# HGRN scores with two levels per product, and the order of the stage around them

## What is computed

```python
def step(S, xs):
    qq, kk, lf, vv = xs
    A = jnp.cumsum(lf, axis=2)
    o_inter = jnp.einsum('bhtd,bhde->bhte', qq * jnp.exp(A), S)
    rel = jnp.where(tri[:, :, None], A[:, :, :, None, :] - A[:, :, None, :, :], -jnp.inf)
    att = jnp.einsum('bhtd,bhsd,bhtsd->bhts', qq, kk, jnp.exp(rel))
    o_intra = jnp.einsum('bhts,bhse->bhte', att, vv)
...
ck = jnp.einsum('bcpgd,pde->bcge', kc[:, cidx] + pe_k[:, None, :], w_ck)
cv = jnp.einsum('bcpgd,pde->bcge', vc[:, cidx] + pe_v[:, None, :], w_cv)
```

## Time and profile before

| | |
|---|---|
| runs, median of 3 | 485.43 us (485.16 to 486.59) |
| the profiled execution | 485.57 us |
| its span, first to last instruction | 483.8 us |
| TensorE busy | 475.2 us, 98% |
| TensorE's weight loads | 463.9 us, 96% |
| VectorE | 343.2 us, 71% |
| ScalarE | 264.6 us, 55% |
| GpSimd | 159.1 us, 33% |
| granted TensorE clock | 0.998 |

### The profile page before, as it was taken

One profiled execution on the slowest core, in us unless ns is written; L12 is line 12 of the kernel. 1 busy time (PEld: TensorE's weight loads), 2 busy tenths in 40 slices (PEclk: granted clock), 3 DMA queues, 4 the chain that ended last, 5 costly groups with the idle time before them and its releaser, 6 DMA issues.

```text
span 483.8 us, 9621 instructions
## 1 busy us (share of the span) xinstructions
PE 475.2 (98%) x3948; PEld 463.9 (96%) x3948; DVE 343.2 (71%) x577; ACT 264.6 (55%) x398; POOL 159.1 (33%) x157
## 2 busy tenths in 40 slices
PE   9999999999999999899999999999999999999995
PEld 8999999999999999889999999999999999999995
DVE  4898967798976566797896747878584257655653
ACT  6887744594562737553565346576554245433531
POOL 1074820807100009990256415436745120000000
PEclk9999999999999999999999999999999999999999
DMA  8956634454354755555355343253525536677502
GB/s 297 330 170 192 189 103 143 125 171 142 119 175 122 188 137 166 155 164 184 119 187 162 106 133 113 87 156 107 174 89 173 175 120 192 213 233 246 175 1 87
DMA packets 76006, 76.43 MB, mean 158 GB/s; under 512 B 5759, under 2 KB 74751, under 8 KB 75963
## 3 DMA queue, kind: packets, MB, share of 16 engines
q1 hardware_dynamic: 75675, 75.64, 50.4%
q10 hardware_dynamic: 288, 0.18, 0.2%
HBM read 74.77 MB, written 1.05 MB: 157 GB/s over the span
## 4 chain that ended last, share of the span: by engine, by line
PE 94%; DVE 2%; ACT 2%; issue 1%; DVEq 0%; ACTq 0%
PE ps L997 75%; PE ps L1022 4%; PE ps L1160 3%; PE ps L1111 2%; PE ps L1185 1%; PE ps L1100 1%; PE ps L1179 1%; PE ps L1127 1%; DVE WL L629 1%; PE ps L1023 1%; PE ps L1114 1%; PE ps L1038 1%; PE ps L1129 1%; PE ps L1128 1%; PE ps L1065 1%
## 5 line engine op out<-in xcount | busy, mean ns | idle before, releaser
L997 PE MATMUL ps<-hH,WL 128*128 128x256 f32 x688 | 195.6, 288 | 1.2 <-DVE WL L629 1.2
L997 PE MATMUL ps<-hL,WH 128*128 128x256 f32 x688 | 194.8, 284 | 0.0
L997 PE MATMUL ps<-hH,WH 128*128 128x256 f32 x688 | 194.8, 284 | 0.0
L629 DVE TENSOR_TENSOR WL<-W,WH 128x2048 fp32r<-128x2048 f32 (+1 forms) x66 | 152.9, 2317 | 19.5 <-PE ps L997 17.1
L432 ACT ACTIVATE WH<-W 128x2048 fp32r<-128x2048 f32 (+1 forms) x66 | 124.7, 1889 | 47.9 <-PE ps L997 46.6
L997 PEld LDWEIGHTS ps<-hH,WL 128*128 128x128 f32 x688 | 130.6, 191 | 2.3 <-DVE WL L629 1.4
L997 PEld LDWEIGHTS ps<-hL,WH 128*128 128x128 f32 x688 | 131.8, 192 | 0.8 <-issue 0.7
L997 PEld LDWEIGHTS ps<-hH,WH 128*128 128x128 f32 x688 | 131.7, 191 | 0.0
L394 POOL TENSOR_SCALAR R<-R,st 128x256 f32<-128x256 f32 x32 | 29.2, 924 | 82.1 <-DVE st L804 82.1
L997 PE MATMUL ps<-bH,WL 128*128 128x256 f32 x192 | 54.9, 286 | 0.0
L997 PE MATMUL ps<-bH,WH 128*128 128x256 f32 x192 | 54.3, 283 | 0.0
(11 more groups left out here) (192 smaller groups left out, 779.3 us busy)
## 6 DMA issues: line engine op xcount, KB each, us to landing
W<-w_in SPq DMA_DIRECT2D x48, 1024.0 KB, 5.2
W<-w_branch SPq DMA_DIRECT2D x12, 1024.0 KB, 5.3
W<-w_out SPq DMA_DIRECT2D x4, 1024.0 KB, 5.4
W<-w_in SPq DMA_DIRECT2D x2, 608.0 KB, 3.8
R<-x SPq DMA_DIRECT2D x2, 512.0 KB, 4.6
W<-w_in SPq DMA_DIRECT2D x2, 512.0 KB, 6.7
R<-cmp_w SPq DMA_DIRECT2D x2, 512.0 KB, 8.5
OC<-pool_w SPq DMA_DIRECT2D x4, 256.0 KB, 5.9
```

The lines of the kernel that those rows point to most:

```text
L629: dve.tensor_tensor(slab_view(WL[:, s % 2], s), slab_view(W[:, s % 3], s), slab_view(WH[:, s % 3], s), ALU.subtract).then_inc(s_lo, 1)
L997: mm = pe.matmul(o, l, r, start=(at == 0 if mixed else k0 + k == 0 and j == 0), stop=(at == len(order) - 1 if mixed else k0 + k == KC - 1 ...
```

## The change

- **Scores.** Levels 32 and 16 become one product, and 8 and 4 another (`RADIX`, `STEPS`). With blocks of b = 16 (4) positions, each key is decayed to the end of its own block (`OWN`), and for the queries of each group of four blocks there are six copies (`REACH`): blocks 1, 2, 3 from block 0's, 1's, 2's end, blocks 2, 3 from 0's and 1's, block 3 from 0's. Per unit these are 192 queries. Level 64 keeps its product of 64, the blocks of 4 theirs of 128, level 128 its own, now in `CVD` as `TOP`.
- **Work on the other engines.** GpSimd has as many instructions a pair, over 4096 elements instead of 3584; VectorE's decay products are nine a head instead of seven, its masks six and a copy instead of five.
- **Order.** The decay products of the heads come in the slabs of `MUL_AT`, scans, norms and roots in those of their tables; slabs 12 to 26 are vs, q2, kc, vc, vwk, vw, bv0, bv1, q0, q1, bv2, bv3, ks, kw, q3. In the keys' slabs the low part of the slab after next comes ahead of the read. GpSimd's pair 1 waits for head 0's products.
- **Compression.** ScalarE copies kc and vc as they are into `XB`, with a fifth group that holds the positions (`CROWS` = 75 = 5 x 15); the product then yields the positions' share beside the others. For the keys VectorE adds it (`CKF`), for the values the spreading matrix `SEL` does.
- **Start and end.** The constants go over SP's queue behind the first tokens. The squares and the scaling of the second tokens are shared by VectorE and ScalarE. The first high half is copied and subtracted in two parts. At the end the sum of the first three quarters goes into the root as its bias.

The diff, cut to what is spoken of:

```diff
-LEVELS = (128, 64, 32, 16, 8, 4)
-NLV = len(LEVELS)
-SMALL_K, SMALL_Q = NLV, NLV + 1
+RADIX = (16, 4)
+STEPS = ((0, 3, 1), (3, 2, 2), (5, 1, 3))
...
-    out += [("vwk", 0, "in", C_VW), ("vw", 0, "in", C_VW), ("vs", 0, "in", C_VS), ("q", 2, "in", C_Q + 2 * SLAB),
-            ("kc", 0, "in", C_KC), ("vc", 0, "in", C_VC)]
-    out += [("bv", n, "in", C_BV + n * SLAB) for n in range(4)]
-    out += [("q", n, "in", C_Q + n * SLAB) for n in (0, 1, 3)]
-    out += [("ks", 0, "in", C_KS), ("kw", 0, "in", C_KW)]
+    bv, q = ([(kind, n, "in", col + n * SLAB) for n in range(4)] for kind, col in (("bv", C_BV), ("q", C_Q)))
+    out += [("vs", 0, "in", C_VS), q[2], ("kc", 0, "in", C_KC), ("vc", 0, "in", C_VC)]
+    out += [("vwk", 0, "in", C_VW), ("vw", 0, "in", C_VW)]
+    out += bv[0:2] + q[0:2] + bv[2:4] + [("ks", 0, "in", C_KS), ("kw", 0, "in", C_KW), q[3]]
...
-BY_ACT = ("f", "hq", "hv", "vs", "vw", "bv", "q", "ks", "kw", "silu", "merge", "out")
-BY_DVE = ("kc", "vc", "ks", "kw", "q", "silu", "branch", "out")
+BY_ACT = ("f", "hq", "hv", "vs", "vw", "bv", "kc", "vc", "q", "ks", "kw", "silu", "merge", "out")
+BY_DVE = ("ks", "kw", "q", "silu", "branch", "out")
...
-SCAN_AT = (2, 6, 10, 14)
+SCAN_AT = (2, 5, 8, 13)
+MUL_AT = (7, 10, 11, 14, 15, 18, 19, 22)
+RSTD_AT = (15, 19, 22, 26)
+NORM_AT = (16, 20, 23, 27)
...
+                if i == 0:
+                    sp.dma_start(K[:, K_ID:K_CMASK], consts[:, K_ID:K_CMASK]).then_inc(s_small, 16)
+            sp.dma_start(V[:], small).then_inc(s_small, 16)
...
+                if p == 1:
+                    pool.wait_ge(s_hmul, 1)
...
+                for r, b in enumerate(RADIX):
+                    n = 2 * T // b
+                    av = a2.rearrange("p (n w) -> p n w", w=b)
+                    pool.tensor_tensor(OWN[p % 2][r].rearrange("p h (n w) -> p (h n) w", w=b),
+                                       k2.rearrange("p (n w) -> p n w", w=b),
+                                       av[:, :, b - 1:b].to_broadcast((P, n, b)), ALU.add)
+                    aw = a2.rearrange("p (n j w) -> p n j w", j=4, w=b)
+                    to = REACH[p % 2][r].rearrange("p h (n j w) -> p (h n) j w", j=6, w=b)
+                    for at, count, far in STEPS:
+                        pool.tensor_tensor(to[:, :, at:at + count], aw[:, :, far:4],
+                                           aw[:, :, 0:count, b - 1:b].to_broadcast((P, n // 4, count, b)), ALU.subtract)
...
-                    act.wait_ge(s_cpe, 2)
+                    act.wait_ge(s_ckf, 1)
...
+                elif kind in ("kc", "vc"):
+                    v = 0 if kind == "kc" else 1
+                    for e in range(2):
+                        src = b2[64 * e:64 * e + 64].rearrange("p q (c j k) -> p k q c j", j=CS // 2, k=2)
+                        for k in range(2):
+                            to = XB[64 * k:64 * k + 64, v, :, :, 0:GROUPS].rearrange("p j c (q e) -> p e q c j", e=2)
+                            last = act.activation(to[:, e], src[:, k], ACT.Copy)
+                    last.then_inc(s_read_a, 1)
...
+            act.wait_ge(s_rcp, 1)
+            act.activation(xin[:, 1, 0:D // 2], xin[:, 1, 0:D // 2], ACT.Copy, scale=st_r[:, 1:2]).then_inc(s_xa, 1)
             act.wait_ge(s_first, 16)
-            act.activation(WH[:, 0, 0:FIRST_A, :], W[:, 0, 0:FIRST_A, :], ACT.Copy).then_inc(s_hi0a, 1)
+            act.activation(WH[:, 0, 0:2, :], W[:, 0, 0:2, :], ACT.Copy).then_inc(s_hi0a, 1)
...
+                if c == 2:
+                    act.activation(WH[:, 0, 2:FIRST_A, :], W[:, 0, 2:FIRST_A, :], ACT.Copy).then_inc(s_hi0a, 1)
...
-                act.wait_ge(s_fin_ss, i + 1)
-                act.activation(st_q[:, i:i + 1], st_t[:, i:i + 1], ACT.Sqrt, scale=1.0 / D,
-                               bias=st_eps).then_inc(s_root, 1)
+                act.wait_ge(s_osq, i + 1)
+                act.wait_ge(s_rest, 1)
+                act.activation(st_q[:, i:i + 1], st_o[:, i, 3:4], ACT.Sqrt, scale=1.0 / D,
+                               bias=st_b[:, i:i + 1]).then_inc(s_root, 1)
...
-                    if s == U0 - 2 + 2 * h:
+                    if s == MUL_AT[h]:
...
+                        for r, b in enumerate(RADIX):
+                            qv = HQ[:, h].rearrange("p (n j w) -> p n j w", j=4, w=b)
+                            ev = REACH[e][r][:, hp].rearrange("p (n j w) -> p n j w", j=6, w=b)
+                            for at, count, far in STEPS:
+                                dve.tensor_tensor(ev[:, :, at:at + count], ev[:, :, at:at + count], qv[:, :, far:4],
+                                                  ALU.mult)
...
+                    dve.wait_ge(s_cpe, 2)
+                    dve.tensor_copy(CSB, ps[0:CROWS, 6, 0:HEAD]).then_inc(s_cv, 1)
+                    link(dve.tensor_copy(st_cb, ck_all[:, GROUPS, 0:1]))
+                    dve.tensor_scalar(CKF, ck_out, st_cb, None, ALU.add).then_inc(s_ckf, 1)
+                if s == CK + 1:
...
+                    for r, b in enumerate(RADIX):
+                        c = slice(192 * r, 192 * r + 192)
+                        to = PM[:, u % 2, 0:P].rearrange("p (n j w) -> p n j w", j=4, w=b)
+                        on = K[:, c].bitcast(mybir.dt.uint32).rearrange("p (n j w) -> p n j w", j=6, w=b)
+                        src = ps[:, b0, c].rearrange("p (n j w) -> p n j w", j=6, w=b)
+                        for at, count, far in STEPS:
+                            link(dve.copy_predicated(to[:, :, far:4], on[:, :, at:at + count], src[:, :, at:at + count]))
+                    dve.tensor_copy(PM[0:64, u % 2, 64:P], ps[0:64, b0, 384:448]).then_inc(s_hmask, 1)
...
+            for j in range(2):
+                dve.wait_ge(s_hi0a, j + 1)
+                dve.tensor_tensor(WL[:, 0, 2 * j:2 * j + 2, :], W[:, 0, 2 * j:2 * j + 2, :],
+                                  WH[:, 0, 2 * j:2 * j + 2, :], ALU.subtract).then_inc(s_lo0, 1)
...
+            dve.memset(XB[:, :, :, 2:, GROUPS].rearrange("p v j c -> p (v j) c"), 0.0)
+            for v in range(2):
+                for k in range(2):
+                    h = slice(64 * k, 64 * k + 64)
+                    pos = V[h, V_PEK + CB * v:V_PEK + CB * v + CB].rearrange("p (r j k) -> p k j r", r=2, k=2)
+                    last = dve.tensor_copy(XB[h, v, :, 0:2, GROUPS], pos[:, k])
+            last.then_inc(s_pos, 1)
...
-                if mixing(s - 1):
+                if mixing(s - 1) and SLABS[s][0] != "kw":
                     lo(s + 1)
                 mix(s)
+                keys = SLABS[s][0] in ("ks", "kw")
+                if keys:
+                    lo(s + 2)
...
+                for r in range(2):
+                    pe.matmul(ps[:, b0, 192 * r:192 * r + 192], OWN[e][r][:, hp, t],
+                              REACH[e][r][:, hp, 192 * i:192 * i + 192], start=(r == 0), stop=False)
+                pe.matmul(ps[:, b0, 384:448], HALF[e][:, hp, t], HALF[e][:, hp, P * i + 64:P * i + P],
+                          start=False, stop=True)
+                mm = pe.matmul(ps[:, b0 + 1, P:2 * P], SMALL_K[e][:, hp, t], SMALL_Q[e][:, hp, t],
+                               start=True, stop=(i == 0))
                 if i:
-                    mm = pe.matmul(ps[:, b0 + 1, 0:P], q[:, 0, hp, 0:P], q[:, 0, hp, P:T], start=True, stop=True)
+                    mm = pe.matmul(ps[:, b0 + 1, 0:P], TOP[e][:, hp, 0:P], TOP[e][:, hp, P:T], start=False, stop=True)
...
-                    keys, values = (cpe[:, a, j].rearrange("p g c -> p (g c)") for a in range(2))
+                    r = j // (CS // 2)
+                    keys, values = (XB[:, a, j % (CS // 2), r:r + NCMP].rearrange("p c g -> p (c g)") for a in range(2))
                     end = dict(start=(j == 0), stop=(j == CB // 2 - 1))
-                    mk = pe.matmul(ck_out.rearrange("p g c -> p (g c)"), WC[:, 0, j, :], keys, **end)
-                    mv = pe.matmul(ps[0:GROUPS * NCMP, 6, 0:HEAD], values, WC[:, 1, j, :], **end)
+                    mk = pe.matmul(ps[64:128, 5, 0:CROWS], WC[:, 0, j, :], keys, **end)
+                    mv = pe.matmul(ps[0:CROWS, 6, 0:HEAD], values, WC[:, 1, j, :], **end)
```

More of the change, by code:

```diff
@@ L818, in read @@
                         last = dve.tensor_tensor(other, src, own, ALU.subtract)
-                elif kind in ("kc", "vc"):
-                    v = 0 if kind == "kc" else 1
-                    pos = V[:, V_PEK + CB * v:V_PEK + CB * v + CB].rearrange("p (r j k) -> p r k j", r=2, k=2)
-                    for r in range(2):
-                        win = b2[:, :, CS * r:CS * r + CS * NCMP].rearrange("p q (c j k) -> p k j q c", j=CS // 2, k=2)
-                        to = cpe[:, v, 8 * r:8 * r + 8].rearrange("p j (q e) c -> p e j q c", e=2)
-                        for e in range(2):
-                            h = slice(64 * e, 64 * e + 64)
-                            for k in range(2):
-                                pv = pos[h, r, k].rearrange("p (j q c) -> p j q c", q=1, c=1)
```

(15 more changed lines are left out.)

172 lines of the change are left out of this document (89 added, 83 removed).

## The result

| | before | after |
|---|---|---|
| runs, median | 485.43 us of 5 (485.16 to 486.59) | 495.67 us of 5 (495.48 to 496.61) |
| the profiled execution, its span | 485.57, 483.8 | 495.54, 493.4 |
| granted TensorE clock | 0.998 | 0.995 |

The ratio is 1.0211, 95% interval 1.0196 to 1.0225. The kernel became slower, as forecast, but by 10.2 us instead of 5.5, and 495.67 lies just above the range, which ended at 495.0.

What follows compares the result with a forecast made beforehand. TensorE, busy 98% of 483.8 us, was taken as the bound. Terms -4.0 + 3.6 + 7.1 - 2.2 + 1.2 - 0.2 = +5.5 on the profiled 485.57 gave 491.1, so 490.9 us by the median; range 483.5 to 495.

Steps and rivals of the forecast that it cites:

- scores: TensorE's score products: ten records of 64 queries become four of 192 and two of 64; -4.0 us over 16 slabs.
- VectorE's decay products: Products now finish after TensorE wants them ahead of slabs 11, 15 and 23; +3.6 us, bounds 0 and +9.
- compression: Alternating half-array key and whole-array value products drain TensorE, 0.57 us for each of 16 steps; +7.1 us.
- keys' slabs: TensorE's two waits (1.2 and 1.0 us) behind the keys vanish as low halves are ready; -2.2 us.
- start: VectorE's cast and later work 1.5 us later, plus position copies, make slab 2's low half late; +1.2 us.
- The rival without drain: Compression: half and whole array alternate smoothly, so it costs only +2.0 us; result 485.8 us; chance 0.16.
- the one with the products in time: VectorE's masks are cheaper or TensorE is delayed elsewhere, so the +3.6 us vanishes; 487.3 us; chance 0.12.
- the masks start 2.9 us after tN: Slabs 14 and 22: VectorE's query read delays masks from 1.5 us after TensorE reaches the small products; 1.4 us lost each.
- slab 13's low part beside it hides there: GpSimd's pair 2 decays, about 13 us, end a little ahead of slab 14; costed at nothing.
- just fits: Slab 18: TensorE needs 8.15 us with the sum of squares, VectorE's chain 8.1, so no loss.
- The rival on GpSimd: Pair 3's decays, if 3 us longer, slow head 5's products by 2.7 us, likewise at 14; 493 to 496; chance 0.08.
- unchanged, so earlier norms buy nothing: Start: TensorE begins transposing when its 18 warming matmuls end, so earlier norms gain no time.

Runs made afterwards that it cites:

- experiment 1: The changed kernel with the compression's 16 key products first, then its 16 value products, instead of alternating: 491.6 us against the change's 495.67.
- Experiment 10: The kernel of experiment 9 with the scan of pair 3 in slab 14 instead of 13, as before the change: 483.06 us.
- experiment 3: The changed kernel with slabs q2 and vs exchanged, so VectorE reads the queries one slab earlier: 492.76 us against the change's 495.67.
- Experiment 4: The changed kernel with ten extra float32 matmuls on TensorE ahead of its wait for head 3's decay products before slab 15: 494.21 us against 495.67.
- experiment 5: The changed kernel with ScalarE copying both parts of the first high half before its normalised chunks: 493.07 us against 495.67.
- experiment 6: The changed kernel with the memset and four position copies moved from VectorE's start into slab 12: 493.46 us against 495.67.
- experiment 7: The changed kernel with the two transfers of constants issued by ScalarE again instead of SP: 494.67 us against 495.67.
- experiment 9: Compressed keys' low part one slab sooner, atop the change with grouped compression, earlier decay products, one first copy, later positions, constants on ScalarE (485.35 us): 484.47 us.

## Why the prediction was right and wrong

The sum, term by term, against the two profiled executions:

| term | predicted | found |
|---|---|---|
| scores | -4.0 | 0.24 a slab, -3.8 |
| VectorE's decay products | +3.6 | +5.7 (0.8, 2.6, 0.9, 1.4) |
| the granted clock | none | +1.7 |
| compression | +7.1 | +6.7 |
| keys' slabs | -2.2 | -2.6 |
| start | +1.2 | +2.4 |
| end, and all else behind the keys | -0.2 | -0.6 |

They make +9.5 of the 9.6 us between the spans. The prediction's terms make +5.5: it missed 2.1 us of waiting for the decay products, the 1.7 us of the clock and 1.2 us of the start, and compression, keys and end came out 0.4 better each. That these three offset part of the miss was luck.

**Right.** The records of 192 columns at 0.162 us, the drains in the compression, the low part that is no longer awaited behind the keys, and the waits of 0.8 and 1.4 ahead of slabs 11 and 23. The drain was the largest term and the one that I had from only two rows; a step of the compression measured 0.55 us for the 0.57 worked out, and experiment 1 shows that it was the mechanism. The rival without drain falls with it, the one with the products in time too.

**The decay products ahead of slab 15.** This is the largest of the steps that failed. The step "the masks start 2.9 us after tN" took only the chain from that slab's own scores. The masks started 4.1 us after it and the loss was 2.6 us instead of 1.4, because the scan ahead of them stood beside GpSimd, took 1.8 us longer, and VectorE came 1.2 us late to the read. The prediction had worked out that pair 2's decays end a little ahead of slab 14 and said that "slab 13's low part beside it hides there": it left out the scan, which the change had moved from slab 14 to 13. (The decays took 13.6 us and ended at 102.1, 0.7 into slab 14.) Experiment 10 shows the scan's term, though in a kernel with the products early; experiment 3 shows scan and read together.

**Slab 18 "just fits".** It did not: 0.9 us. The low part there took 3.11 us instead of 2.27 beside GpSimd's last decays of pair 3, which ended at 135.74, 1 us into the instruction (timelines of DVE and POOL):

```profile
134.79 3.11 DVE L665 TENSOR_TENSOR WL<-W,WH 128x2048 fp32r<-128x2048 f32 x1
```

```profile
134.64 1.10 POOL L391 TENSOR_TENSOR R<-R,BR 128x512 f32<-128x512 f32 x1
```
The rival on GpSimd had the right engine and pair; it looked only at the decay products, and these came after.

**The clock** had no term and no rival. In the kernel before the longest wait inside the program was 1.2 us, and the page showed 9 tenths or more in every slice. That a wait of 2.4 us can cost 1.7 more behind it no row there could have told. Experiment 4 shows that the idle time is needed for it; experiments 1, 5 and 6 show that it is not enough.

**The start** was right as far as it went. The cast came at 11.89 (11.5 was worked out), slab 2's low part ended at 23.11 (22.9), and slabs 1 to 8 lost 1.3 us for the 1.2 forecast. The term of +1.2 was too small, with +2.4 measured: the split copy also made slab 0 itself 0.8 us longer, and I had counted it only as work ahead of later slabs (experiment 5); and "unchanged, so earlier norms buy nothing" did not ask whether the norms could come later, as they did behind the constants, by 0.3 us (experiment 7).

**Two terms were not independent.** "-2.2, the two waits" behind the keys holds only while the compression is long. When experiment 1 made it short, 1.0 us was lost again in the gates' slabs, behind a wait of 0.9; experiment 9 removed it by moving other work of VectorE.

## What to carry over

Before products of different shapes are interleaved on TensorE, see whether they fit in the same part of the array: 31 changes of mode cost more here (31 x 0.143 = 4.4 us) than the merged scores saved in 16 slabs (3.8), and grouping the products by shape cost nothing. When work is moved in time, list for each engine what it now runs beside, all of it and not only the step that was moved, since VectorE's instructions took up to four times as long beside GpSimd's (5.03 us for 1.29). Grouped, with the old places of products and scan, the start undone and one low part sooner, this kernel takes 483.06 us, 0.6% less than before. How much of that is the merged scores' is not shown beyond the 0.24 us that each slab is shorter, since no run had the rest of the change without them.
